# One decoder layer on one NeuronCore: the first norm's factor applied after the projections instead of before them

## The chip, the cores and the metric

The kernel runs on one core of one Trainium2 chip, as one launch. The metric is the device time of the whole program in microseconds (us); lower is better. Before the change it is 1993.66 us, the median of 3 runs that lie between 1993.62 and 1993.81.

## The reference, cut to what matters

The program is one layer of a decoder with two mixers side by side. All sizes that matter here: 256 tokens, 2048 model columns, float32.

```python
u = rms_norm(h, mix_norm_pre)          # y = x * rsqrt(mean(x*x) + EPS) * w
proj = u @ w_in                        # 2048 -> c_q|c_kv|k_rope|z|xBC|dt|gate_attn|gate_ssm
attn = mla_branch(c_q, c_kv, k_r, ...) # starts with rms_norm(c_q), rms_norm(c_kv)
ssm  = mamba2_branch(z, xbc, dt_raw, ...)   # causal conv, silu, scan, * silu(z)
mixed = sigmoid(g_attn) * (attn @ w_attn_o) + sigmoid(g_ssm) * (ssm @ w_ssm_o)
h = h + rms_norm(mixed @ w_out)
... then a SwiGLU block and a gated per-layer embedding block, each with its own norms
```

The factor rsqrt(mean(x*x) + EPS) is one number per token. It can be multiplied into x, or into any row of `proj` that belongs to that token.

## The kernel before

Activations are held transposed, as `u` with 16 tiles of 128 model columns by 256 tokens, each as a high part (fp32r, made by ScalarE) and a low part (the rest, made by VectorE). Weights come in chunks of 128 x 1024 float32 into a ring of four slots, `raw`; ScalarE copies a chunk to its high part `whi` (L1351), VectorE subtracts to get the low part `wlo` (L1914), and TensorE multiplies high by high and low (L655), then low by high (L660). A chunk of the state-space part (phase "ssm") is 8 matmuls of 512 columns and 8 of 256. Eight groups of 20 such chunks follow one another ("ssm"), then 16 chunks of the latent projections ("cq"), then the wide phases ("so", "at", "ao" and the rest).

The order on each engine is written out by hand, and every engine works strictly in that order. The same semaphores as ever bind them: `raw_in` (a chunk has landed), `hi_ready` and `lo_ready` (its parts are made), `chunk_done` (TensorE is through with it). SyncE loads chunk n when `lo_ready` says that chunk n - 4 has been read, and ScalarE may overwrite a slot of `whi` when TensorE has finished the chunk that was four earlier.

The program begins with the phase "bc", four chunks of weights of B and C. It needs `u`, so it starts with x: four loads of 128 x 1024 (token block b, column half i: `x_in00` to `x_in11`), the sum of squares of each token (ScalarE L1413, VectorE L2086), its reciprocal root by a start value and one Newton step (L1403 to L1405, L2069 to L2071), the multiplication of x by it in place (L2081 on VectorE, L1418 on ScalarE), transposes on TensorE (L680), and from PSUM the high part of `u` (L1428) and the low part (L2106), both with the norm's weight as scale. TensorE runs products of a zero tile ahead of that (`idle`, L686). VectorE's `tables()` (L2135 to L2152) spreads the small vectors after chunk 3 of "ssm"; its input `dsk` comes by a DMA of GpSimd.

In "ssm" the first group (group 0) is interleaved with chunks for the rotary key and dt (chunks 1, 3, 4 and 6: 12 matmuls of 256 columns, L636 to L638). In each group the sum of the two halves of a result in PSUM is made by ScalarE (a copy, L1452) and VectorE (an addition, L2189, `both`); ScalarE starts the convolution on it (L1459) and VectorE goes on with it (L2200). The gate z gets the same treatment (L1498, L2260) and then a Silu (L1501). TensorE's products for the scan (L785) wait for masks that VectorE multiplies (L2236). In "cq" the sums are L2361, and TensorE waits for the accumulated squares (L2377) before it makes the norms (L976) after chunk 2 of "so".

Of the kernel before, what the change touches and what calls it, by code (L numbers as in the profile page):

```python
# [147 lines left out]
def build(nc, x, p_in, positions, mix_norm_pre, mix_norm_post, w_in, q_norm, w_uq, kv_norm, w_ukv,  # L148
# [17 lines left out]
    END = CONST0 + 7936  # L166
# [32 lines left out]
    st = const("st", [P, 5, 4, 2])  # L199

# [18 lines left out]
    st0 = first("st0", [P, 2, 8])  # L219

# [17 lines left out]
    e = at("e", [P, HPG, 384], E0)  # L238
    sq = at("sq", [P, 4, SEQ], G0 + 32 * 2048)
# [268 lines left out]
    def _(sp):  # L508
        x_view = x.rearrange("(b p) d -> b p d", p=P)
        for b in range(2):  # L510
            for i in range(2):
                cols = slice(1024 * i, 1024 * i + 1024)
                sp.dma_start(x_tok[:, b, cols], x_view[b][:, cols]).then_inc(sem(f"x_in{b}{i}"), 16)
        for slot in range(RING):
            for src, o in zip(source("bc", 0, slot), (0, STATE)):
                sp.dma_start(raw[:, slot, :].rearrange("p (t n) -> p t n", t=4)[:, :, o:o + STATE], src) \
                    .then_inc(raw_in[slot], 16)
# [47 lines left out]
    def _(pool):  # L565
        pool.wait_ge(sem("x_in11"), 16)
# [63 lines left out]
    def _(pe):  # L630
# [70 lines left out]
        pe.wait_ge(sem("xn_d"), 5)
        x_transposed(1, 1)
        pe.wait_ge(sem("xn_a"), 1)
        x_transposed(2, 1)
        pe.wait_ge(sem("pv_ev"), 1)

        for c_ in range(4):
# [19 lines left out]
            last.then_inc(sem("chunk_done"), 1)  # L727

# [7 lines left out]
        def rope_dt_chunk(c_):  # L736
# [7 lines left out]
            last.then_inc(sem("chunk_done"), 1)  # L744

# [51 lines left out]
        def ssm_group(it):  # L797
            head = isinstance(it, int)
            for c_ in range(20):
# [540 lines left out]
    def _(act):  # L1340
# [67 lines left out]
        def x_square(b, i):  # L1408
            act.wait_ge(sem(f"x_in{b}{i}"), 16)
            if b:  # L1410
                act.wait_ge(sem("x_ssq"), 1 + i)
            cols = slice(1024 * i, 1024 * i + 1024 - 512 * i)
            S.activation(sq_tok[:, cols], x_tok[:, b, cols], ACT.Square, accum_out=st0[:, b, 5 * i:5 * i + 1]) \  # L1413
                .then_inc(sem("x_ssq"), 1)

        def x_normed(b, q):
            cols = slice(512 * q, 512 * q + 512)
            S.activation(x_tok[:, b, cols], x_tok[:, b, cols], ACT.Copy, scale=st0[:, b, 4:5]) \  # L1418
                .then_inc(sem("xn_a"), 1)

        def x_high(q):
# [11 lines left out]
        rstd(st0[:, 0, 2:3], st0[:, 0, 3:4], "x", 1, 1.0 / D_MODEL)  # L1433
        x_square(1, 0)
        x_square(1, 1)
        rstd(st0[:, 1, 2:3], st0[:, 1, 3:4], "x", 2, 1.0 / D_MODEL)
        split("bc", 0, 0)
        act.wait_ge(sem("x_r"), 2)
        x_normed(1, 2)
        act.wait_ge(sem("pv_ev"), 1)  # L1440
        x_high(0)
        split("bc", 0, 1)
        x_high(1)
        x_normed(1, 3)
        split("bc", 0, 2)
        x_high(2)
        split("bc", 0, 3)
        x_high(3)
# [6 lines left out]
        def conv_first(it, pair, tiles):  # L1455

            act.wait_ge(sem("raw_sum"), it * 3 + pair + 1)
# [35 lines left out]
        def ssm_side(it, c_):  # L1493
# [5 lines left out]
            if c_ == 3:  # L1499
                act.wait_ge(sem("z_sum"), it)  # L1500
# [69 lines left out]
        def so_gate(it):  # L1570
            group_end("so", it, 15)
            for half in range(2):
                cols = slice(1024 * it + 512 * half, 1024 * it + 512 * half + 512)
                last = S.activation(m[:, :, cols], psum[:, 2 * half:2 * half + 2, :], ACT.Sigmoid)
# [85 lines left out]
        def ao_gate(it):  # L1660
# [3 lines left out]
            for half in range(2):  # L1664
                last = S.activation(sg[:, :, 512 * half:512 * half + 512], psum[:, 2 * half:2 * half + 2, :], ACT.Sigmoid)
# [243 lines left out]
    def _(dve):  # L1909
# [169 lines left out]
        def x_normed(b, q):  # L2079
            cols = slice(512 * q, 512 * q + 512)  # L2080
            V.tensor_scalar(x_tok[:, b, cols], x_tok[:, b, cols], st0[:, b, 4:5], None, ALU.mult) \  # L2081
                .then_inc(sem("xn_d"), 1)

        def x_total(b):
            dve.wait_ge(sem(f"x_in{b}1"), 16)
            link(V.tensor_tensor_reduce(out=sq_tok[:, 1536:2048], in0=x_tok[:, b, 1536:2048],  # L2086
                                        in1=x_tok[:, b, 1536:2048], scale=1.0, scalar=EPS * D_MODEL,
                                        op0=ALU.mult, op1=ALU.add, accum_out=st0[:, b, 1:2]))
            dve.wait_ge(sem("x_ssq"), 2 * b + 2)
            V.tensor_scalar(st0[:, b, 2:3], st0[:, b, 0:1], st0[:, b, 5:6], st0[:, b, 1:2], ALU.add, ALU.add) \  # L2090
                .then_inc(sem("x_ms"), 1)

        def x_rstd(b):
            dve.wait_ge(sem("x_r0"), b + 1)
            newton(st0[:, b, 2:3], st0[:, b, 3:4], st0[:, b, 4:5], "x_r", scale=1.0 / D_MODEL)
            dve.wait_ge(sem("x_r"), b + 1)

        def x_low(q):
# [10 lines left out]

        x_total(0)  # L2110
        x_rstd(0)
        x_normed(0, 0)
        x_normed(0, 1)
        x_total(1)
        x_normed(0, 2)
        dve.wait_ge(sem("pv_mm"), 1)
        V.tensor_copy(pv[:, 0:16], bank(0)[:, 0:16]).then_inc(sem("pv_ev"), 1)
        x_rstd(1)
        x_normed(1, 0)
        x_normed(1, 1)  # L2120
        dve.wait_ge(sem("hi_ready"), num("bc", 0, 0) + 1)
        V.tensor_tensor(wlo[:, 0, 0:512], raw[:, 0, 0:512], whi[:, 0, 0:512].bitcast(F32), ALU.subtract)
        dve.wait_ge(sem("pv_ev"), 1)
        x_low(0)
        V.tensor_tensor(wlo[:, 0, 512:1024], raw[:, 0, 512:1024], whi[:, 0, 512:1024].bitcast(F32), ALU.subtract) \
            .then_inc(sem("lo_ready"), 1)
        x_normed(0, 3)
        for q in range(1, 4):
            x_low(q)
            split("bc", 0, q)  # L2130
# [54 lines left out]
        def add_halves(it, pair, b):  # L2185
# [3 lines left out]
            V.tensor_tensor(t[:, :, :], psum[:, b:b + 2, 0:SEQ], t[:, :, :], ALU.add).then_inc(sem("raw_sum"), 1)  # L2189

# [166 lines left out]
        def add_c_halves(q):  # L2357
# [3 lines left out]
            V.tensor_tensor(t[:, :, :], psum[:, b:b + 2, 0:SEQ], t[:, :, :], ALU.add).then_inc(sem("raw_sum"), 1)  # L2361

# [589 lines left out]
```

## Time and profile before

| | |
|---|---|
| median of 3 runs | 1993.66 us |
| profiled execution, first to last instruction (span) | 1992.0 us |
| TensorE busy | 1979.0 us (99%) |
| VectorE busy | 1668.8 us (84%) |
| ScalarE busy | 1147.6 us (58%) |
| GpSimd busy | 18.9 us (1%) |
| mean granted TensorE clock | 0.999 |

The profile gives no device time of its own for the profiled execution; its span is 1.7 us under the median of the runs, which include what lies before the first and after the last instruction. Matmul records overlap: the next matmul starts before the record of the last one ends, so the distance from start to start is what one costs, not its length.

### The profile page before, as it was taken

How to read it: one execution, taken by the hardware profiler on the slowest of the kernel's cores; microseconds unless marked ns; L12 is line 12 of the kernel's file. 1: busy time of each engine (PE TensorE's matmuls, PEld its weight loads, DVE VectorE, ACT ScalarE, POOL GpSimd, SP SyncE). 2: the span in 40 equal slices, each digit the busy share in tenths (PEclk: the TensorE clock that was granted, in tenths of full speed). 3: DMA queues.
4: the chain of work that ended last, by engine and by line, in shares of the span. 5: the costliest groups of instructions: out<-in, count | busy, mean ns of one | idle time of the engine just before them, and what ended most of it. 6: DMA issues, size and time to landing. Idle time of an engine off the chain costs nothing.

```text
span 1992.0 us, 29428 instructions
## 1 busy us (share of the span) xinstructions
PE 1979.0 (99%) x10149; PEld 1681.0 (84%) x10149; DVE 1668.8 (84%) x2336; ACT 1147.6 (58%) x1482; POOL 18.9 (1%) x37
## 2 busy tenths in 40 slices
PE   9999999999999999999999999999999999999998
PEld 8888888888888888998888888888888888888886
DVE  7788888889888868767777787999999988888887
ACT  6666566666655545565545565556555555555575
POOL 0000000000000000000000000000000000000000
PEclk9999999999999999999999999999999999999999
DMA  8666676666566566545556667666566666766754
GB/s 235 200 191 190 190 206 184 188 192 195 172 207 209 189 203 223 156 132 156 191 191 239 205 207 242 189 202 202 190 201 200 200 201 201 254 201 207 244 189 152
DMA packets 255197, 394.74 MB, mean 198 GB/s; under 512 B 28840, under 2 KB 161440, under 8 KB 252928
## 3 DMA queue, kind: packets, MB, share of 16 engines
q1 hardware_dynamic: 251104, 369.87, 59.7%
q0 software_dynamic: 3824, 23.43, 3.5%
q8 instruction: 58, 0.95, 0.2%
q14 instruction: 35, 0.29, 0.0%
q10 hardware_dynamic: 176, 0.20, 0.0%
HBM read 387.08 MB, written 6.36 MB: 198 GB/s over the span
## 4 chain that ended last, share of the span: by engine, by line
PE 98%; DVE 1%; ACT 0%; DMA 0%; issue 0%; DVEq 0%; SPq 0%; ACTq 0%
PE acc L655 16%; PE acc L851 15%; PE acc L853 15%; PE acc L852 15%; PE acc L660 8%; PE acc L912 6%; PE acc L913 6%; PE acc L914 6%; PE acc L1107 1%; PE acc L785 1%; PE acc L637 1%; PE acc L636 1%; PE acc L638 1%; PE acc L1038 1%; PE acc L1242 0%; PE acc L714 0%
## 5 line engine op out<-in xcount | busy, mean ns | idle before, releaser
L1914 DVE TENSOR_TENSOR wlo<-raw,whi 128x1024 fp32r<-128x1024 f32 (+2 forms) x559 | 662.5, 1205 | 110.8 <-ACT whi L1351 108.3
L1351 ACT ACTIVATE whi<-raw 128x1024 fp32r<-128x1024 f32 (+1 forms) x560 | 572.2, 1044 | 244.4 <-PE acc L853 81.7
L655 PE MATMUL acc<-u,whi 128*128 128x512 f32 x1376 | 328.7, 391 | 0.0
L851 PE MATMUL acc<-whi,u 128*128 128x512 f32 x824 | 323.0, 392 | 0.1
L853 PE MATMUL acc<-whi,u 128*128 128x512 f32 x824 | 320.8, 389 | 0.0
L852 PE MATMUL acc<-wlo,u 128*128 128x512 f32 x824 | 320.6, 389 | 0.0
L655 PEld LDWEIGHTS acc<-u,whi 128*128 128x128 f32 x1376 | 252.7, 188 | 48.8
L851 PE MATMUL acc<-whi,g 128*128 128x512 f32 x520 | 202.8, 390 | 0.1
L853 PE MATMUL acc<-whi,g 128*128 128x512 f32 x520 | 202.4, 389 | 0.0
L852 PE MATMUL acc<-wlo,g 128*128 128x512 f32 x520 | 202.3, 389 | 0.0
L1374 ACT ACTIVATE whi<-raw 128x1024 fp32r<-128x1024 f32 x72 | 76.5, 1062 | 209.9 <-PE acc L914 162.0
L660 PEld LDWEIGHTS acc<-u,wlo 128*128 128x128 f32 x1376 | 178.1, 191 | 8.3 <-issue 1.5
L660 PE MATMUL acc<-u,wlo 128*128 128x256 f32 x1376 | 184.6, 284 | 0.0
L851 PEld LDWEIGHTS acc<-whi,u 128*128 128x128 f32 x824 | 154.7, 188 | 32.8 <-ACT park L1771 0.6
L853 PEld LDWEIGHTS acc<-whi,u 128*128 128x128 f32 x824 | 154.7, 188 | 32.3
L852 PEld LDWEIGHTS acc<-wlo,u 128*128 128x128 f32 x824 | 154.8, 188 | 31.2
L851 PEld LDWEIGHTS acc<-whi,g 128*128 128x128 f32 x520 | 97.7, 188 | 20.9 <-DVE wlo L1914 0.5
L853 PEld LDWEIGHTS acc<-whi,g 128*128 128x128 f32 x520 | 97.6, 188 | 20.3
L852 PEld LDWEIGHTS acc<-wlo,g 128*128 128x128 f32 x520 | 97.6, 188 | 20.0
L1977 DVE TENSOR_TENSOR wlo<-raw,whi 128x1024 fp32r<-128x1024 f32 x72 | 87.6, 1217 | 0.1
L1381 ACT ACTIVATE thi_ff<-tr_ff 128x1024 fp32r<-128x1024 f32 x58 | 60.0, 1053 | 23.6 <-DVE tr_ff L1982 23.6
L1991 DVE TENSOR_TENSOR tlo_ff<-tr_ff,thi_ff 128x1024 fp32r<-128x1024 f32 x58 | 68.2, 1216 | 0.0
(597 smaller groups left out, 2990.8 us busy)
## 6 DMA issues: line engine op xcount, KB each, us to landing
raw<-w_in_in SPq DMA_DIRECT2D x208, 512.0 KB, 3.8
raw<-w_gate_in SPq DMA_DIRECT2D x176, 256.0 KB, 3.0
raw<-w_up_in SPq DMA_DIRECT2D x176, 256.0 KB, 3.3
raw<-w_down_in SPq DMA_DIRECT2D x88, 512.0 KB, 4.6
raw<-w_ssm_o_in SPq DMA_DIRECT2D x64, 512.0 KB, 4.3
raw<-w_in_in SPq DMA_DIRECT2D x64, 256.0 KB, 4.0
raw<-w_attn_o_in SPq DMA_DIRECT2D x32, 512.0 KB, 4.7
raw<-w_out_in SPq DMA_DIRECT2D x32, 512.0 KB, 4.9
```

The costliest lines, as they stand in the source:

```text
L655: return T.matmul(bank(banks[i]), wh[:, j, i * P:i * P + P], src[:, kts[j], :, :].rearrange("p a s -> p (a s)"), start=start and j == 0, s ...
L660: return T.matmul(bank(banks[i])[:, 0:SEQ], wl[:, j, i * P:i * P + P], src[:, kts[j], 0, :], start=False, stop=not lows_first and stop and ...
L851: T.matmul(o, x_hi, wh[:, j, :], start=start, stop=False, skip_group_check=True)
L852: T.matmul(o, x_hi, wl[:, j, :], start=False, stop=False, skip_group_check=True)
L853: return T.matmul(o, x_lo, wh[:, j, :], start=False, stop=stop, skip_group_check=True)
L912: T.matmul(bank(b), xs[0], ws[0], start=start, stop=False, skip_group_check=True)
L913: T.matmul(bank(b), xs[0], ws[1], start=False, stop=False, skip_group_check=True)
L914: return T.matmul(bank(b), xs[1], ws[0], start=False, stop=stop, skip_group_check=True)
L1351: S.activation(whi[:, slot, 0:w], raw[:, slot, 0:w], ACT.Copy).then_inc(sem("hi_ready"), 1)
L1374: S.activation(whi_f[:, inner], raw_f[:, inner], ACT.Copy).then_inc(sem("hi_ready"), 1)
L1914: V.tensor_tensor(wlo[:, slot, 0:w], raw[:, slot, 0:w], whi[:, slot, 0:w].bitcast(F32), ALU.subtract) \
L1977: V.tensor_tensor(wlo_f[:, inner], raw_f[:, inner], whi_f[:, inner].bitcast(F32), ALU.subtract) \
```

## The change

x is transposed as it lands, without its factor, and the first products start from that. The sum of squares is made later, by ScalarE between the chunks 0 to 3 of "ssm"; the factor of both token blocks is then computed at once (`r_x`, one number per token in a partition), put on a diagonal (`r_diag`), and turned by two TensorE products into rows (`r_rows`, 128 x 256, the same row in every partition). From then on VectorE multiplies each sum of PSUM halves by `r_rows`: `both` three times and z once in each of the eight groups of "ssm" work, and `both` four times in "cq". The semaphores `scaled` and `z_scaled` take the place of `raw_sum` and `z_sum` for ScalarE; TensorE still waits for `raw_sum` and `z_sum`. The rotary key and dt get the factor as they leave PSUM, now on VectorE, and the sigmoid gates take `r_x` as the scale of their activation, in four pieces instead of two. The low parts of the second and fourth chunk of "bc" are made by GpSimd. The loads of x and of "bc" are interleaved, and `idle` runs 17 products instead of 26 + 2. In the diff below, the pieces are those of SyncE, GpSimd, TensorE (its `x_rstd_rows` is called after chunk 5 of group 0), ScalarE, and VectorE, in that order.

```diff
-        for b in range(2):
-            for i in range(2):
+        for i in range(2):
+            for b in range(2):
                 sp.dma_start(x_tok[:, b, cols], x_view[b][:, cols]).then_inc(sem(f"x_in{b}{i}"), 16)
-        for slot in range(RING):
-            for src, o in zip(source("bc", 0, slot), (0, STATE)):
+            for slot in range(2 * i, 2 * i + 2):
+                for src, o in zip(source("bc", 0, slot), (0, STATE)):
...
     def _(pool):
+        G = nc.gpsimd
+        for q in (1, 3):
+            w = width("bc", 0, q)
+            pool.wait_ge(sem("hi_ready"), num("bc", 0, q) + 1)
+            pool.wait_ge(sem("lo_ready"), num("bc", 0, q))
+            G.tensor_tensor(wlo[:, q, 0:w], raw[:, q, 0:w], whi[:, q, 0:w].bitcast(F32), ALU.subtract) \
+                .then_inc(sem("lo_ready"), 1)
         pool.wait_ge(sem("x_in11"), 16)
...
+        def x_rstd_rows():
+
+            pe.wait_ge(sem("r_diag"), 1)
+            pe.wait_ge(sem("pv_ev"), 2)
+            for blk in range(2):
+                last = T.matmul(bank(7)[:, SEQ + blk * P:SEQ + blk * P + P], ones, r_diag[:, blk, :],
+                                start=blk == 0, stop=blk == 1)
+            last.then_inc(sem("r_mm"), 1)
...
-        x_square(0, 0)
-        x_square(0, 1)
...
-            if c_ == 9:
-                group_end("ssm", 0, 6)
-                S.activation(kr, bank(6)[:, 0:SEQ], ACT.Copy).then_inc(sem("kr_ev"), 1)
+            if c_ < 4:
+                x_square(c_ // 2, c_ % 2)
+            if c_ == 4:
+                rstd(st0[:, :, 2], st0[:, :, 3], "x", 1)
...
+        def x_rstd_rows():
+            dve.wait_ge(sem("r_mm"), 1)
+            link(V.tensor_copy(r_rows[:, :], bank(7)[:, SEQ:2 * SEQ]))
...
             V.tensor_tensor(t[:, :, :], psum[:, b:b + 2, 0:SEQ], t[:, :, :], ALU.add).then_inc(sem("raw_sum"), 1)
+            dve.wait_ge(sem("raw_sum"), it * 3 + pair + 1)
+            V.tensor_tensor(t[:, :, :], t[:, :, :], by_rows(2), ALU.mult).then_inc(sem("scaled"), 1)
...
                 V.tensor_tensor(z[:, :, :], psum[:, 0:4, 0:SEQ], z[:, :, :], ALU.add).then_inc(sem("z_sum"), 1)
+                dve.wait_ge(sem("z_sum"), it)
+                V.tensor_tensor(z[:, :, :], z[:, :, :], by_rows(4), ALU.mult).then_inc(sem("z_scaled"), 1)
...
         for c_ in range(20):
             split("ssm", 0, c_)
             if c_ == 3:
                 tables()
+                x_total()
+            if c_ == 4:
+                x_rstd()
+            if c_ == 5:
+                x_rstd_rows()
+            if c_ == 9:
+                rotary_dt()
```

VectorE in group 0, from the low part of chunk 4 to the start of the convolution behind chunk 7, as it was before (`both_95` is `both`, a chunk of 128x512 is one for the rotary key and dt):

```order
L1914 TENSOR_TENSOR wlo<-raw,whi 128x512
L1914 TENSOR_TENSOR wlo<-raw,whi 128x1024
L1914 TENSOR_TENSOR wlo<-raw,whi 128x512
L2189 TENSOR_TENSOR both_95<-acc,both_95 128x512
L1914 TENSOR_TENSOR wlo<-raw,whi 128x1024
L2200 SCALAR_TENSOR_TENSOR xs<-both_95,gp_main,xs 128x255 x2
```

The same place in the changed kernel, with the semaphores that each row waits for (`st_77` is `st0`, `both_97` is `both`):

```order
L1914 TENSOR_TENSOR wlo<-raw,whi 128x512 [waits hi_ready,gpm]
L2069 TENSOR_TENSOR st_77<-st_77 128x2 [waits x_r0]
L2070 SCALAR_TENSOR_TENSOR st_77<-st_77 128x2 [waits dve_step]
L2071 SCALAR_TENSOR_TENSOR r_x<-st_77 128x2 [waits dve_step]
L2089 TENSOR_SCALAR r_diag<-cst,r_x 128x128 [waits x_r]
L2089 TENSOR_SCALAR r_diag<-cst,r_x 128x128
L1914 TENSOR_TENSOR wlo<-raw,whi 128x1024 [waits hi_ready]
L2094 COPY r_rows<-acc 128x256 [waits r_mm]
L1914 TENSOR_TENSOR wlo<-raw,whi 128x512 [waits hi_ready,dve_step]
L2183 TENSOR_TENSOR both_97<-acc,both_97 128x512 [waits raw_cp]
L2185 TENSOR_TENSOR both_97<-both_97,r_rows 128x512 [waits raw_sum]
L1914 TENSOR_TENSOR wlo<-raw,whi 128x1024 [waits hi_ready]
```

Between the low parts of chunks 5 and 6 VectorE now waits for `r_mm`, which TensorE gives; the multiplication by `r_rows` stands between the addition and the low part of chunk 7.

TensorE in the changed kernel from chunk 5 (8 + 8 matmuls) to the first products of chunk 6; before, the two products of `r_diag` were not there and the rest was the same:

```order
L665 MATMUL acc<-u,whi 128x512 x8
L670 MATMUL acc<-u,wlo 128x256 x8
L754 MATMUL acc<-r_diag,cst 128x128 x2
L646 MATMUL acc<-u,whi 128x256
L647 MATMUL acc<-u,whi 128x256
L648 MATMUL acc<-u,wlo 128x256
```

The products that release VectorE stand behind all of chunk 5 on TensorE's queue.

## Rows read from the trace of the kernel before

**Rows 1.** The page's first and fourth part: busy time, and the chain that ended last.

```profile
PE 1979.0 (99%) x10149; PEld 1681.0 (84%) x10149; DVE 1668.8 (84%) x2336; ACT 1147.6 (58%) x1482; POOL 18.9 (1%) x37
PE 98%; DVE 1%; ACT 0%; DMA 0%; issue 0%; DVEq 0%; SPq 0%; ACTq 0%
```

**Rows 2.** Windows: us, then busy us of each engine, PEclk, DMA share, GB/s.

```profile
10.00:20.00 10.00, 8.81 (x53) 7.04 (x54) 9.08 (x23) 8.84 (x19) 1.98 (x3) 1.00 0.87 206
200.00:261.00 61.00, 61.00 (x371) 53.46 (x370) 52.97 (x96) 37.83 (x46) 0.53 (x1) 1.00 0.66 192
```

**Rows 3.** Timeline of TensorE: start us, us, line, matmuls, [idle before].

```profile
1.19 7.41 PE L686 MATMUL acc<-warm 128*128 128x128 f32 x52 [1.19 <-DVE warm L2078]
14.91 2.13 PE L714 MATMUL acc<-u,whi 128*128 128x512 f32 x8 [0.45 <-DVE u L2106]
27.62 2.09 PE L655 MATMUL acc<-u,whi 128*128 128x512 f32 x8
...
37.62 2.00 PE L655 MATMUL acc<-u,whi 128*128 128x512 f32 x8
...
40.41 0.28 PE L636 MATMUL acc<-u,whi 128*128 128x256 f32 x1
...
41.85 1.12 PE L660 MATMUL acc<-u,wlo 128*128 128x256 f32 x8
```

**Rows 4.** DMA issues in short windows: queue, count, size, us from issue to landing.

```profile
x_tok<-x_in SPq DMA_DIRECT2D x1, 512.0 KB, 5.1
...
19.02 0.43 SPq L544 DMA_DIRECT2D raw<-w_in_in  x1
...
raw<-w_in_in SPq DMA_DIRECT2D x1, 512.0 KB, 4.1
```

**Rows 5.** Timeline of ScalarE in the head.

```profile
5.95 1.06 ACT L1413 ACTIVATE sq_tok<-x_tok 128x1024 f32<-128x1024 f32 x1 [3.80 <-DMA x_tok<-x_in]
13.69 0.84 ACT L1428 ACTIVATE u<-acc,pv 128x256 fp32r<-128x256 f32 x2 [0.15 <-PE acc L680]
15.57 1.05 ACT L1351 ACTIVATE whi<-raw 128x1024 fp32r<-128x1024 f32 x1
```

**Rows 6.** Timeline of VectorE in the head.

```profile
14.28 1.90 DVE L2106 SCALAR_TENSOR_TENSOR u<-acc,pv,u 128x256 fp32r<-128x256 f32 x4 [0.41 <-ACT u L1428]
18.95 1.21 DVE L1914 TENSOR_TENSOR wlo<-raw,whi 128x1024 fp32r<-128x1024 f32 x1
30.14 0.54 DVE L2135 COPY pv_all<-acc 128x376 f32<-128x376 f32 x1
32.13 0.18 DVE L2210 COPY gp_main<-gp_all 128x30 f32<-128x30 f32 x1
36.28 0.68 DVE L2189 TENSOR_TENSOR both<-acc,both 128x512 f32<-128x512 f32 x1
38.68 2.45 DVE L2200 SCALAR_TENSOR_TENSOR xs<-both,gp_main,xs 128x255 f32<-128x255 f32 x6
```

**Rows 7.** Timeline of one group: VectorE, and TensorE's products of the scan.

```profile
224.02 1.02 DVE L2236 TENSOR_TENSOR e<-e,cbm 128x384 f32<-128x384 f32 x2
241.69 0.69 DVE L2300 TENSOR_TENSOR sq<-sq 128x512 f32<-128x512 f32 x1
255.32 1.22 DVE L2329 TENSOR_TENSOR g<-z,g 128x1024 f32 x1 [1.51 <-ACT g L1491]
...
227.46 2.82 PE L785 MATMUL acc<-e,xdt 128*64 128x256 f32 x32
```

**Rows 8.** Timeline at the end of "cq" and the start of "so".

```profile
558.87 0.43 DVE L2377 TENSOR_TENSOR acc_q<-acc_q,keep 128x256 f32<-128x256 f32 x1
584.04 1.22 DVE L1914 TENSOR_TENSOR wlo<-raw,whi 128x1024 fp32r<-128x1024 f32 x1
...
560.05 1.02 PE L976 MATMUL acc<-acc_q,cst 128*128 128x256 f32 x4
585.45 0.39 PE L851 MATMUL acc<-whi,u 128*128 128x512 f32 x1
```

More of the change, by code:

```diff
@@ L818, in ssm_group @@
                 chunk_in_rows("ssm", it, c_, banks, u, range(4 * k, 4 * k + 4), k == 0, k == 3, k % 2 == 1)
+                if head and c_ == 5:
+                    x_rstd_rows()
                 if head and c_ == 8:
@@ L1429, in x_high @@
                              scale=pv[:, V_MIXPRE + kt:V_MIXPRE + kt + 1]).then_inc(sem("u_hi"), 1)
-        x_square(0, 0)
-        x_square(0, 1)
[L1433 to L1439, printed above, removed]
-        act.wait_ge(sem("pv_ev"), 1)
[L1441 to L1448, printed above, removed]
+                if between and j == 1:
+                    between()
+        act.wait_ge(sem("pv_ev"), 1)
+        x_high(0, lambda: split("bc", 0, 0))
+        for q in range(1, 4):
+            x_high(q)
+            split("bc", 0, q)
         def low_half(it, pair, b):
@@ L1571, in so_gate @@
             group_end("so", it, 15)
-            for half in range(2):
+            for half, blk in itertools.product(range(2), range(2)):
                 cols = slice(1024 * it + 512 * half, 1024 * it + 512 * half + 512)
-                last = S.activation(m[:, :, cols], psum[:, 2 * half:2 * half + 2, :], ACT.Sigmoid)
+                last = S.activation(m[:, blk, cols], bank(2 * half + blk), ACT.Sigmoid, scale=r_x[:, blk:blk + 1])
             last.then_inc(sem("sg_so"), 1)
@@ L1663, in ao_gate @@
                 act.wait_ge(sem("mixed"), 2)
-            for half in range(2):
-                last = S.activation(sg[:, :, 512 * half:512 * half + 512], psum[:, 2 * half:2 * half + 2, :], ACT.Sigmoid)
+            for half, blk in itertools.product(range(2), range(2)):
+                last = S.activation(sg[:, blk, 512 * half:512 * half + 512], bank(2 * half + blk), ACT.Sigmoid,
+                                    scale=r_x[:, blk:blk + 1])
             last.then_inc(sem("sg_ao"), 1)
@@ L2078, in _, with x_total, x_rstd, rotary_dt @@
         V.memset(warm[:, :], 0.0).then_inc(sem("warm_set"), 1)
[L2079 to L2096, printed above, removed]
+        def x_total():
+            dve.wait_ge(sem("x_ssq"), 4)
+            link(V.tensor_tensor(st0[:, :, 4], st0[:, :, 0], st0[:, :, 1], ALU.add))
+            V.tensor_scalar(st0[:, :, 2], st0[:, :, 4], 1.0 / D_MODEL, EPS, ALU.mult, ALU.add).then_inc(sem("x_ms"), 1)
+        def x_rstd():
+            dve.wait_ge(sem("x_r0"), 1)
+            newton(st0[:, :, 2], st0[:, :, 3], st0[:, :, 4], "x_r", dst=r_x[:, :])
+            dve.wait_ge(sem("x_r"), 1)
+            for b in range(2):
+                last = V.tensor_scalar(r_diag[:, b, :], ident, r_x[:, b:b + 1], None, ALU.mult)
+            last.then_inc(sem("r_diag"), 1)
+        def x_rstd_rows():
+            dve.wait_ge(sem("r_mm"), 1)
+            link(V.tensor_copy(r_rows[:, :], bank(7)[:, SEQ:2 * SEQ]))
+        def rotary_dt():
+            group_end("ssm", 0, 6)
+            V.tensor_tensor(kr, bank(6)[:, 0:SEQ], r_rows[:, :], ALU.mult).then_inc(sem("kr_ev"), 1)
+        def by_rows(n):
+            return r_rows[:, :].unsqueeze(1).to_broadcast([P, n, SEQ])
         def x_low(q):
@@ L2108, in x_low @@
                                        u[:, kt, 0, :].bitcast(F32), ALU.mult, ALU.subtract).then_inc(sem("u_lo"), 1)
[L2110 to L2115, printed above, removed]
         dve.wait_ge(sem("pv_mm"), 1)
         V.tensor_copy(pv[:, 0:16], bank(0)[:, 0:16]).then_inc(sem("pv_ev"), 1)
[L2118 to L2122, printed above, removed]
[L2123 to L2128 removed]
+        dve.wait_ge(sem("pv_ev"), 1)
+        for q in range(4):
             x_low(q)
[L2130 removed]
+            if q in (0, 2):
+                if q:
+                    dve.wait_ge(sem("lo_ready"), num("bc", 0, q))
+                split("bc", 0, q)
         def tables():
```

50 lines of the change are left out of this document (23 added, 27 removed).

## The prediction

> **What bounds the kernel now.** I read the page first: TensorE is busy 1979.0 of 1992.0 us and makes up 98% of the chain that ended last [rows 1]. So only TensorE's idle time can be won, and work on another engine costs only where it makes TensorE wait. The windows say where the idle time is: 1.19 of the 10 us from 10 to 20 is idle, and from 200 to 261, one group of "ssm", none is, with VectorE at 52.97 and ScalarE at 37.83 of 61 us [rows 2]. The timeline of the head then gives the places: zero products up to 8.6, the first real product at 14.91, the first chunk of "ssm" at 27.62 [rows 3]. From there on TensorE waits for nothing. The sum has three parts: how much sooner chunk 0 of "ssm" can start, what group 0 then loses by its new waits, and whether the later multiplications reach TensorE.
>
> **The start.** Before, x lands, is squared, gets its factor and is scaled before the last transposes. Now the first two quarters need only `x_in00` and `x_in10`. A load of x of 0.5 MB lands 5.1 us after its issue at 0.88, at 6.0, when ScalarE's square starts [rows 4, 5]. I take 7.3 for the second in line, an estimate: a quarter of the 5.1 us behind the first, since the loads of a queue overlap. Transposes need 0.5 us per quarter and block; ScalarE's first high part can start near 8.4 instead of 13.69 [rows 5]. But ScalarE now puts the high part of weight chunk 0 between its second and third tile, 1.05 us [rows 5], and TensorE needs it: first product at about 10.3 instead of 14.91, 4.6 us sooner.
>
> Little of this arrives. In "bc" ScalarE and VectorE alternate between `u` (four low parts 1.90 [rows 6]) and weights (1.21 [rows 6]), and the last two quarters wait for x loads that now stand behind weights of "bc". Step by step I get the low part of chunk 0 at 12.6, the high products of chunk 1 at 14.6, of chunk 2 at 18.3, of chunk 3 at 21.1, the end of "bc" at 24.2. GpSimd makes the second low part from 13.5 on and TensorE asks for it at 17.4; the fourth from 20.3 on, asked for at 23.0.
>
> What GpSimd takes, no row shows. The same subtraction costs VectorE 1.21 us [rows 6]; that is the lower bound. Up to 3.8 us each it hides behind transposes and high products, with a wait of up to 1.2 us before chunk 0 to absorb the end. I take it as hidden; at four times VectorE's row, 4.8 us, it costs about 1 us for each of the two, 2 us, my upper bound. The Trainium skill ("GPSIMD Engine Reference", Performance versus the Vector engine) measures a float32 tensor_tensor at 1.96 times VectorE's time; by it the price would be an estimated 2.4 us, and the sum stays.
>
> Chunk 0 of "ssm" cannot follow at 24.2: SyncE issues its load at 19.02, behind eleven small loads that it issues as before, and it lands 4.1 us later, at 23.1 [rows 4]. High part 1.06, low part 1.21, and TensorE starts at 25.45 instead of 27.62. **The start wins 2.2 us.**
>
> **Group 0.** A chunk costs TensorE 2.79 us (37.62 to 40.41), one for the rotary key 1.44 (40.41 to 41.85) [rows 3]. From 25.45, chunks 0 to 4 end at 35.35 if none waits. ScalarE adds four squares of 1.25 us (1.06 in [rows 5] and the reading of the accumulator) between chunks 0 to 3, and finishes at 30.9; VectorE does chunk 3, then `tables` (30.14 to 32.13, 2.0 us, [rows 6]), the new total (0.4) and chunk 4 at 33.6. That just reaches TensorE. Then come three Newton steps and two diagonals, 1.0 us in all, before chunk 5, whose low part is ready at 35.8: **0.5 us of waiting.**
>
> The next wait is built in. VectorE runs about two chunks ahead of TensorE. Now it must wait between the low parts of chunks 5 and 6 for products that TensorE makes after chunk 5. TensorE ends chunk 5 at 38.65, makes the two products (0.44), VectorE copies 256 columns out of PSUM (0.4) and makes the low part of chunk 6 (0.68), and TensorE goes on at 40.5: 1.4 us idle. VectorE has lost its lead, and what is queued behind it is the addition (0.68, [rows 6]), the new multiplication (0.69 for 128 x 512 from SBUF, [rows 7]) and the low part of chunk 7 (1.21), against 1.44 us of TensorE for chunk 6: 1.0 us more. Behind that is the convolution (2.45, [rows 6]), held by ScalarE's start of it, which now waits for `scaled`, and the low part of chunk 8, against 2.79 us: 0.7 us. At chunk 9 VectorE is ahead again. **Group 0 loses 0.5 + 1.4 + 1.0 + 0.7 = 3.6 us, and 0.4 for the two products, 4.0.** Head in all: +1.8 us.
>
> **The later groups.** A multiplication is a two-input pass from SBUF: 0.69 us for 512 columns and 1.22 for 1024 [rows 7]. Three and one per group make 3.3 us, 27 us over eight groups, and VectorE has 8 us idle per group [rows 2]. What counts is the lead at each place. z's multiplication delays Silu, a table load and ScalarE's chunk 4; VectorE is 1.3 us late there, 0.9 after its own idle time, and 1.6 with the first multiplication of `both` ahead of chunk 7. The last masks then end at 226.6 instead of 225.0, and TensorE wants them at 227.46 [rows 7]: 0.8 us are left. The two other multiplications come where VectorE waits for ScalarE or TensorE, and at the group's end it waited 1.51 us for ScalarE's `g` anyway [rows 7], so nothing is carried on. **0 us.**
>
> **"cq" and "so".** The last multiplication lies on a chain: sum, high part, square, accumulation, end at 559.30; TensorE begins the norms' products at 560.05, its weight load 0.25 sooner [rows 8]. 0.7 us more makes it late by 0.1 to 0.3. VectorE carries the 0.7 us on without idle time of its own up to chunk 12 of "so", whose low part ends at 585.26 while TensorE starts on it at 585.45 [rows 8]: together **0.5 us**. The sigmoids split in four have several chunks of room.
>
> **The sum.** -2.2 + 4.0 + 0 + 0.5 = +2.3 us on a span of 1992.0; the median of the runs is 1.7 above that span, so 1993.66 becomes about 1996.0. A change under 0.2% (4.0 us) is about what a measurement of this kernel can't tell from none: I forecast no change that can be told, on the slow side.
>
> **Rivals.** *The head keeps its gain.* If the two products came sooner, or the work behind chunk 6 overlapped better than in a strict sum, the losses at chunks 7 and 8 (1.7) and 0.5 at chunk 5 fall away: +0.1, 1993.7; with the norms' products still in time 1993.2. For it: TensorE's start at 10.3 leaves slack in "bc"; against it: the order on VectorE's queue. 0.2. *The whole 4.6 us arrives*, because chunk 0 of "ssm" lands sooner and VectorE never starves TensorE: 1989 to 1990. Against it is the load at 19.02. 0.05.
>
> *The masks come late* (slower). The multiplications with a broadcast operand may cost more than plain ones; from 1.4 times on, the 0.8 us before L785 are gone. At twice the price the delay is 3.5 against 2.4 us of room: 1.1 us in each of groups 1 to 7, +7.7, 2003.7. For it: three delays in a row on one chain with ScalarE in between; against it: L2300 and L2329 are of the same kind and cheap. 0.13.
>
> *The head's clock or GpSimd* (slower). Fewer zero products, then transposes with gaps of 0.5 and 1.7 us: if the granted clock fell to 1.2 GHz, products of "bc" would take twice as long. Before, TensorE was idle for 1.19 of the 10 us after 10.0 and PEclk stayed at 1.00 [rows 2]. Three microseconds at half speed cost 1.5, less 1.2 of waiting before chunk 0; all of "bc" at half speed costs 11 us less 1.2, 2006. With GpSimd's upper bound, 1997 to 2006. 0.1. The Trainium skill ("TensorE: Matmul & The Clock Gate", Part 4: PE-mode transpose) says that transposes don't count as TensorE being busy in the same way, which speaks for this rival; before, transposes stood in the same place and PEclk stayed at 1.00.
>
> My forecast itself, 1994.5 to 1997.6, has 0.52.
>
> **How the numbers follow.** The range is 1991.2 to 1999.8: below it lies most of the second rival (0.05), above it the third and the costly half of the fourth (0.15 or so together). Faster by over 0.2% (below 1989.7): 0.05. Slower by over 0.2% (above 1997.6): masks 0.13, clock and GpSimd 0.06, the upper tail of my own sum 0.04: 0.23. Within: 0.72.
>
> **What would show it.** First L716 near 10.3, first L665 near 25.5, the copy of `r_rows` (L2094) after a wait for TensorE, TensorE idle before L646 of chunk 6 (1.4) and before chunks 7 and 8. L2185 at 0.69 with room left before the scan's products; TensorE at 61 of 61 us in a later group. A wait at the norms' products or chunk 12 of "so" under 1 us. I am wrong if TensorE idles in the later groups, if GpSimd's subtraction takes over 4 us, if PEclk leaves 1.00, or if VectorE's wait for `r_mm` finds TensorE done already.

## Result, and the profile after

The changed kernel takes 1997.07 us (median of 21 runs, 1996.58 to 1997.62), the kernel before 1993.98 us in the same session (1993.56 to 1995.70). The ratio is 1.0015 with a 95% interval of 1.0009 to 1.0021: 3.1 us slower. That is clear of zero and under the 0.2% taken as the bound of "no change", which the upper end of the interval just passes. The profiled execution has a span of 1995.4 us against 1992.0. Line numbers are now those of the changed kernel and differ by up to 14 from those of before.

The page's first and fourth part, after, against [rows 1]:

```profile
PE 1979.4 (99%) x10131; PEld 1679.6 (84%) x10131; DVE 1689.7 (85%) x2360; ACT 1147.1 (57%) x1485; POOL 23.4 (1%) x39
PE 96%; DVE 3%; ACT 1%; DMA 0%; issue 0%; DVEq 0%; ACTq 0%
```

TensorE has the same work (1979.4 against 1979.0). VectorE has 20.9 us more, but the span grew by 3.4 only, so most of it is hidden; its share of the chain went from 1% to 3%, and this is what there is to find. The windows, with the columns of [rows 2]:

```profile
10.00:20.00 10.00, 8.79 (x53) 7.53 (x54) 7.72 (x16) 8.35 (x18) 2.38 (x1) 1.00 0.74 218
200.00:261.00 61.00, 61.00 (x374) 53.59 (x373) 55.90 (x100) 38.28 (x47) 0.53 (x1) 1.00 0.65 189
```

In a later group TensorE is busy for 61.00 of 61 us as before, with 2.9 us more on VectorE; PEclk is 1.00 in both. The view of waits of TensorE (us in total, times, longest), whole:

```profile
PE acc L716 <- ACT whi L1365: 1.5, 1, 1.5
PE acc L646 <- DVE wlo L1914: 1.2, 1, 1.2
PE acc L697 <- DVE warm L2078: 1.2, 1, 1.2
PE acc L665 <- DVE wlo L1914: 1.1, 2, 0.6
PE acc L670 <- DVE wlo L1914: 0.8, 1, 0.8
PE acc L865 <- DVE wlo L1914: 0.4, 1, 0.4
PE acc L725 <- DVE wlo L1914: 0.2, 1, 0.2
PE acc L865 <- ACT park L1771: 0.2, 1, 0.2
```

All but L865 stand in the first 50 us. TensorE's timeline there, against [rows 3]:

```profile
10.97 2.12 PE L716 MATMUL acc<-u,whi 128*128 128x512 f32 x8 [1.55 <-ACT whi L1365]
...
24.52 0.49 PE L735 MATMUL acc<-cst,rows 104*128 104x104 f32 x4
25.64 2.14 PE L665 MATMUL acc<-u,whi 128*128 128x512 f32 x8 [0.63 <-DVE wlo L1914]
...
35.66 2.00 PE L665 MATMUL acc<-u,whi 128*128 128x512 f32 x8
...
38.46 0.60 PE L754 MATMUL acc<-r_diag,cst 128*128 128x128 f32 x4
40.30 0.39 PE L646 MATMUL acc<-u,whi 128*128 128x256 f32 x1 [1.24 <-DVE wlo L1914]
...
42.77 1.22 PE L670 MATMUL acc<-u,wlo 128*128 128x256 f32 x8 [0.76 <-DVE wlo L1914]
...
46.27 2.11 PE L665 MATMUL acc<-u,whi 128*128 128x512 f32 x8 [0.45 <-DVE wlo L1914]
```

The first product comes 3.9 us sooner and chunk 0 of "ssm" 2.0 us sooner (25.64 against 27.62). What sets chunk 0 is its load, for which ScalarE waits:

```profile
23.19 1.06 ACT L1365 ACTIVATE whi<-raw 128x1024 fp32r<-128x1024 f32 x1 [2.50 <-DMA raw<-w_in_in]
```

Further on, chunk 6 at 40.30 is level with before (40.41), chunk 7 is 0.9 us late and chunk 9 is 1.7 us late. VectorE's timeline says why:

```profile
39.10 0.42 DVE L2094 COPY r_rows<-acc 128x256 f32<-128x256 f32 x1 [3.80 <-PE acc L754]
39.56 0.69 DVE L1914 TENSOR_TENSOR wlo<-raw,whi 128x512 fp32r<-128x512 f32 x1
40.16 0.68 DVE L2183 TENSOR_TENSOR both<-acc,both 128x512 f32<-128x512 f32 x1
40.88 0.69 DVE L2185 TENSOR_TENSOR both<-both,r_rows 128x512 f32<-128x512 f32 x1
41.49 1.22 DVE L1914 TENSOR_TENSOR wlo<-raw,whi 128x1024 fp32r<-128x1024 f32 x1
42.63 2.45 DVE L2196 SCALAR_TENSOR_TENSOR xs<-both,gp_main,xs 128x255 f32<-128x255 f32 x6
```

VectorE stands still for 3.80 us until TensorE has made the two products behind chunk 5, and the low parts that TensorE wants next stand behind that copy.

In the later groups nothing moves. The last masks are ready before TensorE wants them, here in group 3:

```profile
227.41 1.02 DVE L2232 TENSOR_TENSOR e<-e,cbm 128x384 f32<-128x384 f32 x2
...
229.21 2.82 PE L797 MATMUL acc<-e,xdt 128*64 128x256 f32 x32
```

Behind the groups there are three places: the norms' products and chunk 12 of "so" (+0.8 us together; TensorE's starts are then 2.5 us later than before), and the products of L926 to L928 in pass 0 of "ao", called the sevens below (+0.5). The gate there, on ScalarE, before and after, and the two weight loads of TensorE that wait behind it:

```profile
967.98 1.94 ACT L1665 ACTIVATE sg<-acc 128x1024 f32<-128x1024 f32 x2
...
970.71 2.42 ACT L1664 ACTIVATE sg<-acc,r_x 128x512 f32<-128x512 f32 x4
973.00 2.02 ACT L1395 ACTIVATE thi_ao<-tr_ao 128x1024 fp32r<-128x1024 f32 x2
973.18 0.19 PEld L926 LDWEIGHTS acc<-whi,g 128*128 128x128 f32 x1 [0.47 <-ACT sg L1664]
975.39 0.19 PEld L926 LDWEIGHTS acc<-thi_ao,xa_new 128*128 128x128 f32 x1 [0.28 <-DVE tlo_ao L1991]
```

Before, the gate took 1.94 us in two instructions. Small shifts make up the rest of the 3.4 us: 0.2 near 607 us and 0.14 near 1131 us. One place differs between executions for no reason that an edit gives: near 1175 us e4, whose edit is in the first 26 us, loses 0.9 us, the changed kernel none. So the span of a single execution does not settle tenths; TensorE's starts ahead of a place and behind it do better.

### The profile page after: what moved, and what is told of

Read it like the earlier page. It is cut to its first block, busy times and chain, and to the rows that moved or that the text cites. A ratio compares the mean times of both kernels' runs of the same rounds, so it can differ in the third digit from the quotient of the medians.

```text
span 1995.4 us, 29429 instructions
## 1 busy us (share of the span) xinstructions
PE 1979.4 (99%) x10131; PEld 1679.6 (84%) x10131; DVE 1689.7 (85%) x2360; ACT 1147.1 (57%) x1485; POOL 23.4 (1%) x39
## 4 chain that ended last, share of the span: by engine, by line
PE 96%; DVE 3%; ACT 1%; DMA 0%; issue 0%; DVEq 0%; ACTq 0%
PE acc L665 16%; PE acc L865 15%; PE acc L866 15%; PE acc L867 15%; PE acc L670 8%; PE acc L926 6%; PE acc L927 6%; PE acc L928 6%; PE acc L1121 1%; PE acc L797 1%; PE acc L647 1%; PE acc L646 1%; PE acc L648 1%; DVE wlo L1914 1%; PE acc L1052 1%; PE acc L1256 0%
## 5 line engine op out<-in xcount | busy, mean ns | idle before, releaser
L1914 DVE TENSOR_TENSOR wlo<-raw,whi 128x1024 fp32r<-128x1024 f32 (+1 forms) x558 | 661.9, 1206 | 108.4 <-ACT whi L1365 106.4
L865 PE MATMUL acc<-whi,u 128*128 128x512 f32 x824 | 323.2, 392 | 0.5 <-DVE wlo L1914 0.4
L865 PE MATMUL acc<-whi,g 128*128 128x512 f32 x520 | 202.8, 390 | 0.1
L670 PEld LDWEIGHTS acc<-u,wlo 128*128 128x128 f32 x1376 | 178.1, 191 | 9.3 <-issue 1.5
L670 PE MATMUL acc<-u,wlo 128*128 128x256 f32 x1376 | 184.7, 284 | 0.8 <-DVE wlo L1914 0.8
L865 PEld LDWEIGHTS acc<-whi,u 128*128 128x128 f32 x824 | 154.7, 188 | 33.6 <-DVE wlo L1914 1.1
L865 PEld LDWEIGHTS acc<-whi,g 128*128 128x128 f32 x520 | 97.6, 188 | 20.8 <-DVE wlo L1914 0.5
```

The lines of the kernel that those rows point to most:

```text
L670: return T.matmul(bank(banks[i])[:, 0:SEQ], wl[:, j, i * P:i * P + P], src[:, kts[j], 0, :], start=False, stop=not lows_first and stop and ...
L865: T.matmul(o, x_hi, wh[:, j, :], start=start, stop=False, skip_group_check=True)
L1914: V.tensor_tensor(wlo[:, slot, 0:w], raw[:, slot, 0:w], whi[:, slot, 0:w].bitcast(F32), ALU.subtract) \
```

## Experiments

Ten kernels; e11 is made from the kernel before, the others from the changed one. The times of before in their sessions were 1993.82 to 1993.97, so times of different rows can be compared to about 0.2 us; the runs of one kernel spread over 1 to 2 us.

| kernel | median us | ratio to before (95%) | span |
|---|---|---|---|
| changed kernel | 1997.07 | 1.0015 (1.0009 to 1.0021) | 1995.4 |
| e1 rows early | 1994.29 | 1.0001 (0.9992 to 1.0010) | 1992.7 |
| e2 two sigmoids | 1996.90 | 1.0016 (1.0007 to 1.0025) | 1995.1 |
| e3 no cq factor | 1996.60 | 1.0013 (1.0004 to 1.0022) | 1994.4 |
| e4 VectorE's lows | 1997.15 | 1.0016 (1.0007 to 1.0025) | 1995.9 |
| e5 load early | 1996.08 | 1.0012 (1.0003 to 1.0021) | 1994.2 |
| e6 twice | 2008.26 | 1.0070 (1.0056 to 1.0084) | 2006.6 |
| e8 e1, e2 and e5 | 1993.08 | 0.9996 (0.9987 to 1.0005) | 1991.3 |
| e9 no group factor | 1997.15 | 1.0015 (1.0006 to 1.0024) | 1995.8 |
| e10 loads as before | 1999.49 | 1.0026 (1.0016 to 1.0036) | 1997.8 |
| e11 before, new loads | 1999.98 | 1.0030 (1.0018 to 1.0043) | 1998.1 |

### e1: the two products one chunk sooner

```diff
                 if rope_dt("ssm", it, c_):
                     rope_dt_chunk(c_)
+                    if c_ == 4:
+                        x_rstd_rows()
                     continue
...
-                if head and c_ == 5:
-                    x_rstd_rows()
```

> TensorE makes the two products of r_diag behind chunk 4 of group 0 in place of chunk 5; nothing else moves. Theory (the three waits before chunks 6, 7 and 8 come from VectorE waiting 3.8 us for TensorE to end chunk 5): r_diag is ready before chunk 4 ends at 35.7, VectorE waits about 1 us and keeps a lead, and the waits of 1.24, 0.76 and 0.45 us before L646, L670 and L665 go; 2.4 us less than the changed kernel, about 1994.6, ratio to the kernel before 1.0003. Rival (VectorE and ScalarE have simply more work in the head than they can do in 50 us, wherever the products stand): the waits move to chunks 7 to 10 and the time stays at 1997 within 0.5.

1994.29 us, 2.8 us less than the changed kernel. VectorE's timeline of e1:

```profile
34.57 1.22 DVE L1914 TENSOR_TENSOR wlo<-raw,whi 128x1024 fp32r<-128x1024 f32 x1
36.61 0.42 DVE L2094 COPY r_rows<-acc 128x256 f32<-128x256 f32 x1 [0.82 <-PE acc L754]
37.07 0.69 DVE L1914 TENSOR_TENSOR wlo<-raw,whi 128x512 fp32r<-128x512 f32 x1
```

The wait of 3.80 us is 0.82, L646 and L670 are gone from the view of waits, and TensorE is 2.47 us earlier from chunk 9 on, although chunk 0 started 0.3 us later in this execution: 2.8 us, as the medians say. The same work on VectorE and ScalarE, with nothing in another place but two matrix products (four records), is 0.1% faster: the theory holds and the rival is out. What is left of group 0's loss of 3.7 us is 0.9; the two products are 0.4 of it, and one wait of 0.17 us remains at chunk 8.

### e2: the gates in two instructions

```diff
-            for half, blk in itertools.product(range(2), range(2)):
-                last = S.activation(sg[:, blk, 512 * half:512 * half + 512], bank(2 * half + blk), ACT.Sigmoid,
-                                    scale=r_x[:, blk:blk + 1])
+            for blk in range(2):
+                last = S.activation(sg[:, blk, :].rearrange("p (h n) -> p h n", h=2), psum[:, blk:4:2, :],
+                                    ACT.Sigmoid, scale=r_x[:, blk:blk + 1])
```

and the same in `so_gate`.

> The gates' sigmoids in so and ao as two instructions of 1024 columns (one for each block of tokens, its factor as the scale) in place of four of 512. Theory (ScalarE is 0.5 us later at its place in the queue by the two additional instructions, and TensorE's sevens in pass 0 of ao wait for it): ACT L1664 back from 2.42 to about 1.95 us, the waits of 0.47 and 0.28 us at L926 fall to those of before (0.15), the offset of TensorE to the kernel before stays at +2.7 past 1017 us; 0.5 to 0.7 us less, about 1996.4. Rival (the sums of the sevens are late for another reason, by the position of the loads): nothing moves, 1997.1.

```profile
970.43 2.12 ACT L1665 ACTIVATE sg<-acc,r_x 128x1024 f32<-128x1024 f32 x2
```

The gate takes 2.12 us, not 1.95, the wait for it falls from 0.47 to 0.17 while that of 0.28 stays at 0.31, and TensorE gains 0.27 us there by its starts, and 0.2 at the gate of "so". The medians differ by 0.17 us, which these runs can't tell from none. The direction is right by the profile; the gain was under the 0.5 to 0.7 us that I expected, and the second wait stayed.

### e3: no factor on the four sums of "cq"

```diff
         def add_c_halves(q):
...
-            V.tensor_tensor(t[:, :, :], t[:, :, :], by_rows(2), ALU.mult).then_inc(sem("scaled"), 1)
```

with ScalarE's `split_c` waiting for `raw_sum`.

> The four sums of the cq chunks are not multiplied by the rstd of x (that factor is left out of c_q and c_kv). Theory (the multiplication of the last sum lies on the chain that ends in the norms' products, and what VectorE carries on reaches chunk 12 of so): TensorE's offset to the kernel before stays at +1.8 past 560 us and L990 and L865 wait for nothing or as before; 0.6 us less, about 1996.4. Rival (the offset of 0.6 us at 560 to 587 us comes from something other than the multiplications): 0.

L990 starts at 561.47 in place of 561.83, the wait of 0.37 us at L865 is gone from the view, and TensorE's offset to the changed kernel goes from -0.32 ahead of L990 to -1.07 behind chunk 12: 0.75 us, as the theory has it. The medians give 0.5.

### e4: low parts two and four on VectorE again

The loop over `q in (1, 3)` leaves GpSimd, and VectorE calls `split("bc", 0, q)` for all four.

> Low parts of the second and fourth B/C chunk made by VectorE again, everything else as changed. Theory (GpSimd's 2.38 us are hidden and VectorE has the 1.2 us too, since transposes and high products cover both): 0 within 0.3 us, the first L665 within 0.3 us of 25.64. Rival 1 (GpSimd's subtraction ends late and costs): 1 us or more less. Rival 2 (VectorE needs GpSimd's help): 0.5 to 1.2 us more in front of L725 or L735.

1997.15 us, and the first "ssm" product at 25.59 against 25.64. TensorE came to its first product 0.8 us later in this execution, and from there the phase "bc" took as long as in the changed kernel (13.55 us to L735 in both). Who makes these two low parts is worth nothing here, in either direction; both rivals are out. In the changed kernel GpSimd took 2.38 and 2.39 us:

```profile
14.09 2.38 POOL L574 TENSOR_TENSOR wlo<-raw,whi 128x1024 fp32r<-128x1024 f32 x1 [13.51 <-ACT whi L1365]
20.77 2.39 POOL L574 TENSOR_TENSOR wlo<-raw,whi 128x1024 fp32r<-128x1024 f32 x1 [4.30 <-ACT whi L1365]
```

### e5: the load of chunk 0 sooner

```diff
-        for v, n, at_row in vec:
+        for k, (v, n, at_row) in enumerate(vec):
+            if k == 1:
+                sp.wait_ge(sem("lo_ready"), num("ssm", 0, 0) - RING + 1)
+                for src, o in zip(source("ssm", 0, 0), (0, P)):
+                    sp.dma_start(raw[:, 0, 0:width("ssm", 0, 0)].rearrange("p (t n) -> p t n", t=src.shape[1])
+                                 [:, :, o:o + src.shape[2]], src).then_inc(raw_in[0], 16)
             sp.dma_start(rows[at_row:at_row + n, 0, :], v.rearrange("(t p) -> t p", p=P)) \
...
```

and the later loop over the loads leaves this chunk out.

> The load of chunk 0 of ssm is issued behind the first of the eleven loads of rows in place of behind all of them, 4 us earlier. Theory (ScalarE's split of chunk 0 waits 2.5 us for that transfer and TensorE 0.63 us for its low part): first L665 no longer waits, starts 0.6 us earlier at 25.0, and the waits behind it stay, as they hang on TensorE's own chunk 5; 1996.5. Rival (the rows then land too late for L735, or the B/C chunks' transfers share the queues and come later): 0 or up to +1.

```profile
13.48 0.41 SPq L527 DMA_DIRECT2D raw<-w_in_in  x1
...
24.33 2.10 PE L671 MATMUL acc<-u,whi 128*128 128x512 f32 x8
```

Issued at 13.48 in place of 17.88. Chunk 0 starts at 24.33, 1.3 us sooner, and the median is 1.0 us lower. Of the 1.3 us, 0.5 are there from the first transpose on, because TensorE was through its zero products sooner in this execution (they took 5.68 us against 6.17); 0.8 are the load's. The theory gave 0.6; the waits behind chunk 5 stayed, as it said.

### e6: every multiplication at double price

```diff
             V.tensor_tensor(t[:, :, :], t[:, :, :], by_rows(2), ALU.mult).then_inc(sem("scaled"), 1)
+            dve.wait_ge(sem("scaled"), it * 6 + (2 * pair + 1))
+            V.tensor_tensor(t[:, :, :], t[:, :, :], t[:, :, :], ALU.max).then_inc(sem("scaled"), 1)
```

and the same for `z`.

> Behind each multiplication by r_rows in the eight ssm groups (three sums of pairs and z) a second pass of VectorE over the same tile that changes no value (maximum of the tile with itself), so that the price of the factor is doubled: 0.69 and 1.22 us more each. Theory (sum of the prediction: three delays on one chain make 3.5 us against 2.4 us of room before the scan's products): L797 waits 1.1 us in each of the groups 1 to 7, 7.7 us more than the changed kernel, about 2004.7 and a little more in the head. Rival (the idle time of VectorE, 8 us per group, takes all of it): under 1 us more. At double price the room is told from zero either way.

2008.26 us, 11.2 more. The view of TensorE's waits of e6 is headed by a line that neither kernel has:

```profile
PE acc L797 <- DVE e L2234: 6.1, 7, 0.9
```

and TensorE's timeline shows one of the seven:

```profile
234.16 2.82 PE L797 MATMUL acc<-e,xdt 128*64 128x256 f32 x32 [0.87 <-DVE e L2234]
```

At double price the masks are late, 0.87 us in each of the groups 1 to 7 where I had worked out 1.1. But a group costs 1.4 us, not 0.87: TensorE's starts shift by 0.97 at the scan's products, by another 0.3 at the first products of chunk 8 and by 0.13 at those of chunk 16. The place is right, and the double price does exceed the room; 7.7 us was too little because I had looked at one wait only.

### e9: no multiplications in groups 1 to 7

```diff
-            V.tensor_tensor(t[:, :, :], t[:, :, :], by_rows(2), ALU.mult).then_inc(sem("scaled"), 1)
+            if isinstance(it, int):
+                V.tensor_tensor(t[:, :, :], t[:, :, :], by_rows(2), ALU.mult).then_inc(sem("scaled"), 1)
```

and none of `z` (the factor is missing there).

> The factor of x's norm is left out of the sums of pairs in the ssm groups 1 to 7 and of all of z (some 25 us less work for VectorE); group 0, cq and everything else as changed. Theory (these multiplications are hidden in VectorE's idle time, with room left before the scan's products): the starts of TensorE's instructions from 48 to 530 us are those of the changed kernel, time 1997.1 within 0.4. Rival (they cost TensorE something that no wait shows, by ports or by transfers that start later): 0.5 us or more faster, growing group by group.

1997.15 us, against 1997.07: between 48 and 560 us the distance to the changed kernel's starts is constant. So 29 multiplications, 20.5 us of VectorE's busy time (1669.2 against 1689.7), are worth nothing, while in e6 32 further passes, 25.1 us of busy time, cost 11 us.

### e10 and e11: the norm and the order of the loads apart

e10 puts the four transfers of x ahead of all eight of the B/C chunks again; e11 is the kernel before with the changed kernel's order.

```diff
-        for i in range(2):
-            for b in range(2):
+        for b in range(2):
+            for i in range(2):
                 cols = slice(1024 * i, 1024 * i + 1024)
                 sp.dma_start(x_tok[:, b, cols], x_view[b][:, cols]).then_inc(sem(f"x_in{b}{i}"), 16)
-            for slot in range(2 * i, 2 * i + 2):
-                for src, o in zip(source("bc", 0, slot), (0, STATE)):
+        for slot in range(RING):
+            for src, o in zip(source("bc", 0, slot), (0, STATE)):
```

> The four transfers of x stand ahead of all eight of the B/C chunks again, as in the kernel before; the transposes, products and GpSimd as changed. It tells how much of the start's gain of 4 us at the first product comes from leaving out the norm and how much from the order of the loads. If the loads' order carries part of it: B/C chunk 0 lands about 3.1 us later (two transfers of 1.6 us stand ahead of it), the first product starts at 13 to 14 in place of 10.97, chunk 0 of ssm about 2 us later and the end 1.5 to 2 us later, 1999. Rival (what comes behind, loads of chunk 0 at 17.9 and GpSimd, sets the start of chunk 0 anyway): first product late but chunk 0 within 0.5 of 25.64, time 1997.1 to 1997.5.

> The kernel before, with the changed kernel's order of the first loads alone (first halves of x, two B/C chunks, second halves of x, the other two); x is still normed before it is transposed. Theory (the order pays only where the transposes do not wait for the norm: a block's norm wants its second half of x, which now stands behind four transfers of 256 KB and lands some 3 us later): first product 2 to 4 us later than 14.9, chunk 0 of ssm 1 to 3 us later than 27.6, time 1995 to 1997. Rival (the order of the loads alone brings the gain of 2 us, the norm costs the start nothing): chunk 0 near 25.6, time near 1992.

ScalarE and TensorE of e10, and its windows (columns of [rows 2]; the granted clock stands ahead of the last two numbers):

```profile
12.02 1.06 ACT L1365 ACTIVATE whi<-raw 128x1024 fp32r<-128x1024 f32 x1 [1.53 <-DMA raw<-w_in_in]
13.18 3.65 PE L716 MATMUL acc<-u,whi 128*128 128x512 f32 x8 [3.19 <-ACT whi L1365]
...
12.00:14.00 2.00, 0.82 (x2) 0.76 (x3) 0.53 (x2) 1.98 (x4) 0.00 (x0) 0.81 1.22 290
14.00:16.00 2.00, 2.00 (x6) 1.54 (x6) 2.00 (x4) 2.00 (x5) 0.00 (x0) 0.50 1.18 279
16.00:18.00 2.00, 2.00 (x15) 1.81 (x14) 1.05 (x3) 0.21 (x1) 1.70 (x1) 0.83 0.29 76
```

VectorE and TensorE of e11:

```profile
12.23 0.69 DVE L2086 CUSTOM_DVE_ANT_0 sq_tok<-x_tok 128x512 f32<-128x512 f32 x1 [11.10 <-DMA x_tok<-x_in]
14.98 1.97 PE L680 MATMUL acc<-cst,x_tok 128*128 128x128 f32 x8 [5.61 <-DVE x_tok L2081]
```

In e10 the first product starts at 13.18 and chunk 0 of "ssm" at 28.01, 2.4 us later than in the changed kernel and 0.4 later than the 27.62 of before; the median is 2.4 us higher. The start now waits for weights in place of x, as the first theory has it. But the wait has a second price that the expectation did not have: TensorE stood idle for 3.19 us, the granted clock fell to 0.50, the lower of its two levels, and the eight first products took 3.65 us in place of 2.12. From the first product to chunk 0 it took 14.83 us, against 13.83 in e4, where TensorE comes to chunk 0 without a wait as well. So about 1.0 of the 2.4 us is the clock's; without it chunk 0 would have started near 27.0, an estimate from these two numbers.

In e11 the norm waits for the second half of x, squared at 12.23 in place of 7.30 (the first half at 5.95, as in [rows 5]), and TensorE is 5.7 us late at chunk 0 and stays so; the median is 6.1 us higher. I had expected 1 to 3 us. The direction is right and the size is not: the second half of x comes 4.9 us later, not 3, and here too the clock fell (0.50 from 14 to 18 us, behind 5.61 us of idle TensorE), so that the first eight transposes took 1.97 us in place of 1.09. As they were measured, neither half of the change pays alone, and both together bring 2.0 us. How much each would be worth at full clock no run shows.

### e8: e1, e2 and e5 together

> The three edits together: products of r_diag behind chunk 4, two sigmoids, load of chunk 0 early. If each is independent as the theories have it, 2.4 + 0.6 + 0.6 = 3.6 us less than the changed kernel, 1993.4, ratio to the kernel before 0.9997. Rival (they share one slack: VectorE has no lead to take up the earlier start of chunk 0): about 2.4 less, 1994.6.

1993.08 us, 4.0 less than the changed kernel. Its waits of TensorE, whole:

```profile
PE acc L722 <- ACT whi L1371: 1.5, 1, 1.5
PE acc L703 <- DVE warm L2085: 1.2, 1, 1.2
PE acc L871 <- DVE wlo L1921: 0.3, 1, 0.3
PE acc L731 <- DVE wlo L1921: 0.3, 1, 0.3
PE acc L671 <- DVE wlo L1921: 0.2, 1, 0.2
PE acc L871 <- ACT park L1778: 0.2, 1, 0.2
```

The gains add up (2.8 + 0.2 + 1.0). It is the fastest kernel here, 0.9 us under before, but the interval of its ratio holds 1: not shown to be faster.

## Why the prediction was right, point by point

The forecast was 1996.0 us in a range of 1991.2 to 1999.8 and "no change that can be told, on the slow side"; 1997.07 came out, with a ratio whose interval ends at 1.0021, just above the 1.002 that I had called no change.

- **The start, -2.2.** Measured -1.98. First product at 10.97, not 10.3, since ScalarE's first high part came at 9.09, not 8.4; chunk 0 at 25.64 against 25.45. The load of chunk 0 sets it, as argued: ScalarE waits 2.50 us for it, and e5 moves the start by moving the load. That the landing came out right is in part luck: I had it issued at 19.02 and landing 4.1 us later; it was issued at 17.88 and took 5.3. What I had not seen is that the missing norm brings the gain only together with the new order of the loads (e10, e11).
- **GpSimd, hidden.** 2.38 us by the trace, 1.97 times VectorE's 1.21 [rows 6]; e4 shows the choice of engine to be worth nothing. The Trainium skill ("GPSIMD Engine Reference", Performance versus the Vector engine) measures a ratio of 1.96 for a float32 tensor_tensor, and the trace agrees.
- **Group 0, +4.0.** Measured: chunk 9 at +1.74 from -1.98, so 3.7. Its idle parts: 1.24 for 1.4, 0.76 for 1.0, 0.45 for 0.7, and 0 for the 0.5 at chunk 5, where VectorE's low part ended at 35.30 and TensorE came at 35.66 (in e9, where ScalarE waited 1.06 us for a load at 29.59, that wait did appear, with 0.42). The records of matmuls overlap, so from start to start the three waits cost more than the idle time shown, 1.5, 1.0 and 0.7 us, and the two products 0.4. The 1.4 of the prediction is 0.3 more than the terms it names for it (0.4 and 0.68). The cause, VectorE's wait for products that TensorE makes one chunk too late, is shown by e1.
- **The later groups, 0.** Right, and so is the room: the last masks of the group end at 228.43 and L797 starts at 229.21, 0.8 us later, as worked out. e9 shows the zero directly, e6 that doubling the price is too much.
- **"cq" and "so", +0.5.** 0.8 by TensorE's starts, 0.75 by e3: the right places, a little dearer than worked out.
- **"The sigmoids split in four have several chunks of room."** This step failed. ScalarE's next instructions are the high parts of `tr_ao` and TensorE's sevens stand right behind them; the gate itself, too, is waited for (0.47 us). Measured +0.5 us in "ao", of which e2 gives back 0.27, and +0.2 in "so" at 607 us, which it gives back.
- **The sum.** +2.3 forecast, +3.4 by the spans and +3.1 by the medians. TensorE's offset to before is +1.74 behind the head (forecast +1.8) and +2.5 behind chunk 12 of "so" (forecast +2.3); behind that I had nothing, and there came 0.2 in "so", 0.5 in "ao" and 0.14 near 1131 us.
- **The rivals.** The masks came late where the price is doubled, not at 0.69. The clock stayed at 1.00 through the head: between 10 and 20 us TensorE was busy for 8.79 us, and its longest pause behind the transposes was 1.55 us. The rival was not far off, though: in e10 the same 16 transposes and a pause of 3.19 us were followed by a granted clock of 0.50, for about 1.0 us. The Trainium skill ("TensorE: Matmul & The Clock Gate", Part 4: PE-mode transpose) says that transposes don't count as TensorE being busy in the same way. In the changed kernel 16 transposes (1.97 us) and the pause behind them did not lower the granted clock; whether the transposes had a part in e10's fall no run shows.

## What to carry to other kernels

Where one engine's queue waits in order for a small result of the engine that it feeds, ask what stands behind the wait: two small products one chunk too late cost 2.8 us here, nearly all that the change lost, and moving them is free. Before paying for a shorter chain at the start, look at what lands when: taking work out of the chain (e10) and reordering the transfers (e11) made the start 0.4 and 5.7 us later alone, and 2 us sooner together. And look at the granted clock of every variant: about 1 us of e10's loss is the clock, which fell while TensorE waited. Idle time of VectorE is not a price list: 20 us were free and the next 25 cost 11, so find the one place with the least room (here 0.8 us before the scan's products) and count against that.

## What the runs showed of the hardware

The gate in "ao", a sigmoid of 2048 columns out of PSUM by ScalarE: two instructions of 1024 took 1.94 us without a scale and 2.12 with a column as the scale, read from two banks that don't adjoin; four of 512 took 2.42. So 0.15 us for each additional instruction, and some 0.1 each for the other form, of which the runs don't tell whether the scale or the banks is the cause.

The first of SyncE's eleven small loads took 2.58 us to issue in the changed kernel, 2.52 in e5 and 2.51 in e11, but 0.83 before and in e10, where the large transfers ahead of it stood in the other order and it began 1.8 to 1.9 us later. In all five its issue ended between 13.4 and 13.7 us. Each of the next eight took 0.25 to 0.5. Why is open.

TensorE's granted clock fell to 0.50 in e10 behind 3.19 us of idle TensorE and in e11 behind 5.61 us; it stayed at 1.00 behind pauses of 1.55 us in the changed kernel and 1.29 before. At the very start TensorE's zero products follow one another at 0.21 us and later at 0.11 us, while the profile's clock says 1.00 for both. The step came at 4.1 us in the execution of before, at 5.6 in the changed kernel's and at 7.3 in e4's, and the 34 records took 5.68 us in e5, 6.17 in the changed kernel and 6.96 in e4. So the first transposes move by some tenths from one execution to the next, whatever the kernel.
